# A transformer kernel on one core: head 0's first query is made before the norm's root, the modulation tiles move forward, and the first picks take other slots

## What is computed

```
mod = silu(c) @ w_ada + b_ada                      # 6 parts of 1024: shift1, scale1, gate1, shift2, scale2, gate2
h = rms_norm(x, norm1_w) * (1 + scale1) + shift1
... projections, indexed attention, short convolution -> y_mix
x = x + gate1 * (y_mix @ w_out)
h2 = rms_norm(x, norm2_w) * (1 + scale2) + shift2
# the experts, for each token and each of 8 heads:
q = h2 @ peer_wq; s = q @ subkeys                  # two halves of 128 scores
the 16 best of each half, the 16 best of their 256 sums -> 16 experts; g = softmax(of the 16 sums)
a = gelu(peer_u[expert] . h2); x += gate2 * sum(g * a * peer_v[expert])
```

## Time and profile before

| | us |
|---|---|
| three runs | 1177.68, 1178.76, 1179.75 |
| median | 1178.76 |
| the profiled execution | 1180.36 |
| its span, first to last instruction | 1178.4 |
| lies around the span | 1.96 |

### The profile page before, as it was taken

How to read it: one execution, slowest core, us unless ns; L and a number is a source line. 1 busy time by engine, 2 the same in 40 slices (tenths; PEclk the granted TensorE clock), 3 DMA queues, 4 the chain that set the end, 5 groups by cost and what they waited for, 6 DMA issues and landing times.

```text
span 1178.4 us, 18884 instructions
## 1 busy us (share of the span) xinstructions
PE 1051.1 (89%) x7587; PEld 980.2 (83%) x7587; DVE 837.5 (71%) x1801; ACT 433.0 (37%) x913; POOL 268.8 (23%) x289
## 2 busy tenths in 40 slices
PE   8999987999999987777877778878999999999997
PEld 6999986998899877777877777778899888898886
DVE  7978889667667667666776766655756868765776
ACT  3635832123212221222122122211557654476452
POOL 1000005343334333333333333434000000300000
PEclk9999999999999999998999999989999999999999
DMA  9965988999999999999999999999854655455540
GB/s 371 406 244 180 348 313 307 420 421 420 421 420 420 421 420 421 420 421 420 420 420 421 420 421 422 420 422 420 325 208 161 237 205 184 147 211 179 186 171 36
DMA packets 59480, 390.35 MB, mean 331 GB/s; under 512 B 6785, under 2 KB 7809, under 8 KB 15618
## 3 DMA queue, kind: packets, MB, share of 16 engines
q0 software_dynamic: 36864, 268.45, 55.0%
q1 hardware_dynamic: 21056, 120.10, 27.8%
q10 hardware_dynamic: 1474, 0.60, 0.2%
HBM read 388.08 MB, written 1.05 MB: 330 GB/s over the span
## 4 chain that ended last, share of the span: by engine, by line
PE 63%; DMA 24%; DVE 6%; ACT 4%; issue 1%; SPq 0%; another core or an unknown queue 0%; DVEq 0%; ACTq 0%
DMA rows<-in_peer_uv,work 23%; PE aux L1566 23%; PE pj L1609 6%; PE pj L1611 5%; PE pj L1610 5%; PE aux L1545 5%; PE pj L1286 5%; PE pj L1287 4%; PE pj L1288 4%; DVE rows L2061 2%; DMA rows<-in_w_ada 1%; PE aux L1360 1%; ACT work L1142 1%; ACT rows L1010 1%; PE aux L1425 1%
## 5 line engine op out<-in xcount | busy, mean ns | idle before, releaser
L1566 PE MATMUL aux<-work,rows 128*128 128x128 f32 x2080 | 263.4, 291 | 73.8 <-ACT work L1142 73.8
L1566 PEld LDWEIGHTS aux<-work,rows 128*128 128x128 f32 x2080 | 256.2, 206 | 81.6 <-ACT work L1142 81.4
L1566 PE MATMUL aux<-work,low_pairs 128*128 128x128 f32 x2016 | 238.2, 279 | 30.2 <-ACT work L1142 30.1
L1566 PEld LDWEIGHTS aux<-work,low_pairs 128*128 128x128 f32 x2016 | 233.0, 195 | 34.0 <-ACT work L1142 34.0
L898 POOL DMA_INDIRECT rows<-in_peer_uv,work x130 | 125.5, 965 | 301.2 <-PE aux L1566 232.1
L707 DVE TENSOR_TENSOR wlo<-wring,whi 128x1024 fp32r<-128x1024 f32 x100 | 121.0, 1235 | 77.6 <-ACT whi L701 77.1
L898 POOL DMA_INDIRECT low_pairs<-in_peer_uv,work x126 | 118.3, 939 | 158.5 <-PE aux L1566 153.4
L1286 PE MATMUL pj<-xh,whi 128*128 128x256 f32 x512 | 146.3, 286 | 0.4
L1137 ACT ACTIVATE work<-work 128x4 f32<-128x4 f32 (+2 forms) x71 | 14.7, 207 | 358.3 <-DVE work L2061 358.3
L1287 PE MATMUL pj<-xl,whi 128*128 128x256 f32 x512 | 144.8, 283 | 0.0
L1288 PE MATMUL pj<-xh,wlo 128*128 128x256 f32 x512 | 144.8, 283 | 0.0
(11 more groups left out here) (288 smaller groups left out, 1461.5 us busy)
## 6 DMA issues: line engine op xcount, KB each, us to landing
wring<-in_w SPq DMA_DIRECT2D x76, 1024.0 KB, 4.8
rows<-in_w_ada SPq DMA_DIRECT2D x40, 512.0 KB, 10.1
low_pairs<-in_w_ada SPq DMA_DIRECT2D x1, 4096.0 KB, 13.4
rows<-in_w SPq DMA_DIRECT2D x3, 1024.0 KB, 10.4
rows<-in_peer_uv,work POOLq DMA_INDIRECT x130
work<-in_late_rows SPq DMA_DIRECT2D x2, 1024.0 KB, 7.5
xT<-in_gate_rows SPq DMA_DIRECT2D x2, 1024.0 KB, 7.2
rows<-in_norm_rows SPq DMA_DIRECT2D x2, 1024.0 KB, 7.3
```

The lines of the kernel that those rows point to most:

```text
L1566: ins = mm(peer_sum[t][:, c * P:(c + 1) * P], pair(n)[:, D + c * P:D + (c + 1) * P], diag[:, n % PICKS, :], start=(n % (EXPERT_HEADS * PIC ...
```

## The change

1. `early_scores_of_head_0` is cut up. ACT makes `xT` times the gain (`times_gain`) as soon as a column of `xT` is there; PE multiplies these by head 0's query weights (`early_products`), before the root is known. DVE forms the query as product times inverted root plus the shift's part. The shift's part is made earlier: 16 products of one column (`shift_queries`), placed on PE between `sum_v` of tile 1 and `turn_y` of tile 0.
2. `second_norm` becomes one DVE multiplication of 1024 columns for each token tile, and it stands behind `route(0)`. Head 1 gets an early query too. The root for the gate's softmax is made per token (`token_sums`, `token_rms`), used in `route_pairs(0)` and `gate_exps(0)`.
3. Forty-six modulation tiles come through the ring of slots, seven more of them before the additions to `xT` begin; the last load has two tiles. The bias and gain are made before these additions.
4. The first round of picks takes slots in the order 0, 1, 6, 7, 9, 10, 11, 2, 3, 4, 8, 5 (`FIRST_ORDER`), and so do all rounds up to pick 239; picks 240 and up use n % 12 again.

```diff
-ADA_AFTER = {4: range(16, 21), 7: (21, 22), 8: (23, 24), 9: (25, ), 13: range(26, 29), 18: range(29, 34), 22: (34, ), 20: (35, ), 25: (36, 37), 27: (38, 39)}
+ADA_AFTER = {4: range(16, 21), 7: (21, 22), 8: (23, 24), 9: (25, ), 12: range(26, 31), 13: range(31, 34), 14: (34, 35), 18: range(36, 41), 22: (41, ), 20: (42, ),
+             25: (43, 44), 27: (45, )}
+RING_TILES = 46
...
+FIRST_ORDER = (0, 1, 6, 7, 9, 10, 11, 2, 3, 4, 8, 5)
+LAST_ROUND = LAST_PICK // SLOTS * SLOTS - SLOTS
+def slot(n):
+    return n % SLOTS if n >= LAST_ROUND else FIRST_ORDER[n % SLOTS]
+def pick_ahead_in_slot(n):
+    return max(m for m in range(n - 2 * SLOTS, n) if m >= 0 and slot(m) == slot(n))
...
-                    sp.wait_ge(sums, 1 + NT)
+                    sp.wait_ge(sums, 2 + NT)
...
+                    if n >= SLOTS:
+                        pool.wait_ge(pair_used, pick_ahead_in_slot(n) + 1)
+                    elif k in FIRST_QUERY_SLOTS:
+                        pool.wait_ge(queries, 2 * FIRST_QUERY_SLOTS.index(k) + 2)
+                    elif k == KEYS_SLOT:
                         pool.wait_ge(expert_scores, 2)
-                    if n == LAST_ADA_SLOT:
-                        pool.wait_ge(last_ada_used, KC)
-                    if n >= SLOTS:
-                        pool.wait_ge(pair_used, n - SLOTS + 1)
+                    elif k in (LAST_ADA_SLOT, CONDITION_SLOT):
+                        pool.wait_ge(last_ada_used, LAST_TILES)
...
+            def times_gain(t, c):
+                nc.scalar.activation(hT[:, c, halves_[t]], xT[:, c, halves_[t]], ACT.Copy, scale=gain[:, c:c + 1]).then_inc(gained, 1)
...
+            act.wait_ge(sums, 2 + NT)
+            nc.scalar.activation(token_rms[:, :], aux[:, 1, 0:1], ACT.Sqrt, bias=eps[:, 0:1], scale=1.0 / D).then_inc(std_ready, 1)
+            for c in range(KC):
+                times_gain(1, c)
+            shift(0)
             shift(1)
...
             sum_v(att1, pt_buf, v_of_head, tiles=(1, ))
+            first_query = UNITS_1.index(queries_of(0))
+            w_wait(pe, first_query)
+            pe.wait_ge(mod_ready, 2 * KC + 2)
+            pe.wait_ge(att1["y_out"], 1)
+            for s in range(2):
+                for k in range(KC):
+                    ins = mm(aux[:, 0, s:s + 1], w_slot(first_query)[:, k, s * P:(s + 1) * P], mod[:, 3 * KC + k:3 * KC + k + 1],
+                             start=(k == 0), stop=(k == KC - 1))
+            ins.then_inc(shift_queries, 1)
             turn_y(att1, ytok, tiles=(0, ))
...
-            out_sums(4, 5)
-            out_sums(6, 7)
+            out_sums(4, 5, tiles=(0, ))
+            early_products(*range(6))
+            out_sums(6, 7, tiles=(0, ))
+            early_products(6, 7)
+            out_sums(*range(4, KC), tiles=(1, ))
...
-            keep_busy(4, 1)
-            early_scores_of_head_0()
+            early_scores_of(0)
+            token_sums()
             pe.wait_ge(taken_dve, KC)
+            pe.wait_ge(h_ready, 2 * KC)
             turn_h2(0)
+            early_query_of_head_1()
+            early_scores_of(1)
             pe.wait_ge(h_ready, 3 * KC)
             score_query(0)
...
+            low_to(12)
+            ada_dots(21, 26)
             low_to(14)
...
+            for s in range(2):
+                dve.wait_ge(early_query, s + 1)
+                v.scalar_tensor_tensor(pq[:, 0, s, 0:P], rstd[:, 0:P], shift_query[:, s:s + 1], aux[:, 4 + s, 0:P], ALU.mult, ALU.add) \
+                    .then_inc(early_query_out, 1)
+            second_root(0)
...
             route(0)
+            for t in range(NT):
+                second_norm(t)
+                if t == 0:
+                    second_root(1)
             last_ada_tiles()
```

More of the change, by code:

```diff
@@ L1104, in score_out @@
                 act.wait_ge(expert_scores, h + 1)
-                first = 1 if h == 0 else 0
+                first = 1 if h < EARLY_HEADS else 0
                 nc.scalar.copy(s_all[:, h + first * EXPERT_HEADS::EXPERT_HEADS, :],
                                aux[:, h % 2, first * 2 * KEYS:].rearrange("p (n k) -> p n k", k=2 * KEYS)).then_inc(scores_out, 1)
-            shift(0)
-            for s in range(2):
-                act.wait_ge(early_query, s + 1)
-                nc.scalar.copy(pq[:, 0, s, 0:P], aux[:, 4 + s, 0:P]).then_inc(early_query_out, 1)
             act.wait_ge(early_scores, 1)
             nc.scalar.copy(s_all[:, 0, :], aux[:, 0, 0:2 * KEYS]).then_inc(early_scores_out, 1)
-            shift(1)
+            act.wait_ge(sums, 2 + NT)
[3 more added lines that the diff above has]
+            shift(0)
+            shift(1)
+            for s in range(2):
+                act.wait_ge(early_query, 2 + s + 1)
+                nc.scalar.copy(pq[:, 1, s, 0:P], aux[:, 4 + s, 0:P]).then_inc(early_query_out, 1)
+            act.wait_ge(early_scores, 2)
+            nc.scalar.copy(s_all[:, 1, :], aux[:, 1, 0:2 * KEYS]).then_inc(early_scores_out, 1)
             def gate_exps(g):
                 act.wait_ge(routed, g + 1)
-                nc.scalar.activation(gate[g % EXPERTS], top, ACT.Exp, bias=negtop, accum_out=gate_sum[g % EXPERTS]).then_inc(gate_exp, 1)
-            for h in range(AHEAD + 1):
-                score_query(h)
-                score_out(h)
-                if h:
-                    gate_exps(h - 1)
+                nc.scalar.activation(gate[g % EXPERTS], top, ACT.Exp, bias=negtop, scale=token_rms[:, 0:1] if g == 0 else 1.0,
+                                     accum_out=gate_sum[g % EXPERTS]).then_inc(gate_exp, 1)
+            score_query(0)
+            gate_exps(0)
+            score_out(0)
+            score_query(1)
+            score_out(1)
+            gate_exps(1)
+            score_query(2)
+            score_out(2)
             def x0_hi(t):
@@ L1512, in _, with out_sums @@
                 ins.then_inc(proj, 1)
-            def out_sums(*columns):
+            def out_sums(*columns, tiles=range(NT)):
                 for k in columns:
-                    for t in range(NT):
+                    for t in tiles:
                         pe.wait_ge(squares, k + 1 if k < KC - 1 else KC + t)
@@ L1525, in _, with early_products, token_sums @@
             whole(mixed_in, 2)
-            out_sums(4, 5)
-            out_sums(6, 7)
+            def early_products(*columns):
+                for k in columns:
+                    pe.wait_ge(gained, k + 1)
+                    for s in range(2):
+                        ins = mm(aux[:, 4 + s, 0:P], w_slot(first_query)[:, k, s * P:(s + 1) * P], hT[:, k, 0:P], start=(k == 0), stop=(k == KC - 1))
+                        if k == KC - 1:
+                            ins.then_inc(early_query, 1)
+            def token_sums():
+                pe.wait_ge(att1["y_out"], NT)
+                for k in range(KC):
+                    ins = mm(aux[:, 1, 0:1], sq[:, k, 0:P], ones[:, 0:1], start=(k == 0), stop=(k == KC - 1))
+                ins.then_inc(sums, 1)
+            out_sums(4, 5, tiles=(0, ))
[3 more added lines that the diff above has]
+            out_sums(*range(4, KC), tiles=(1, ))
             def turn_h2(t):
@@ L1555, in score_keys @@
                     pe.wait_ge(scores_out, h - 1)
-                for t in range(1 if h == 0 else 0, NT):
+                if h < EARLY_HEADS:
+                    pe.wait_ge(early_scores_out, h + 1)
+                for t in range(1 if h < EARLY_HEADS else 0, NT):
                     for s in range(2):
@@ L1778, in second_gain, with second_root, second_norm @@
                 chain.link(v.tensor_scalar(gain[:, :], part(4), 1.0, None, ALU.add))
-                chain.link(v.tensor_tensor(gain[:, :], gain[:, :], cols[:, N2W:N2W + KC], ALU.mult))
-            def second_norm():
-                for t in range(NT):
-                    ts = slice(t * P, (t + 1) * P)
-                    dve.wait_ge(std_ready, 2 + t)
-                    chain.link(v.reciprocal(rstd[:, ts], rstd[:, ts]))
-                    for c in range(KC):
-                        v.scalar_tensor_tensor(hT[:, c, ts], xT[:, c, ts], gain[:, c:c + 1], rstd[:, ts], ALU.mult, ALU.mult).then_inc(h_scaled, 1)
+                v.tensor_tensor(gain[:, :], gain[:, :], cols[:, N2W:N2W + KC], ALU.mult).then_inc(mod_ready, 1)
+            def second_root(t):
+                dve.wait_ge(std_ready, 2 + t)
+                chain.mark(v.reciprocal(rstd[:, t * P:(t + 1) * P], rstd[:, t * P:(t + 1) * P]))
+            def second_norm(t):
+                ts = slice(t * P, (t + 1) * P)
+                dve.wait_ge(gained, (t + 1) * KC)
+                chain.wait()
+                v.tensor_tensor(hT[:, :, ts], hT[:, :, ts], rstd[:, ts].unsqueeze(1).broadcast_to([P, KC, P]), ALU.mult).then_inc(h_scaled, 1)
             for z, x_in in zip((slice(0, HC), slice(HC, KC)), x_loaded):
@@ L1968, in _ @@
             y_low(1)
-            ada_dots(3 * KC + ADA_RING + 2, 4 * KC)
-            ada_dots(4 * KC, 4 * KC + 1)
-            late = 4 * KC
+            ada_dots(38, 40)
```

(2 more changed lines are left out.)

100 lines of the change are left out of this document (55 added, 45 removed).

## The result

The changed kernel takes 1196.73 us (median of 4 runs, 1196.48 to 1199.83) against 1178.96 us for the kernel before: ratio 1.0155, 95% interval 1.0143 to 1.0168. That is 17.8 us slower, where 10.0 were forecast and the range ended at 1194.5. Its profiled execution took 1196.72 us with a span of 1194.8, so the span grew by 16.4 us. The other 1.4 us lie in the kernel before: its profiled execution took 1180.36 us, 1.4 above its own median, that of the changed kernel its median. In what follows, "later" means: than the same instruction of the kernel before, in the two profiled executions.

The account below looks back on a forecast made before the run. Transfer and PE's loop were taken as coupled, the loop's later start setting the end: 11.7 + 1.5 + 1.0 - 5.0 + 0.8 = +10.0 us, median 1188.8 us, range 1184.3 to 1194.5.

Parts of the forecast that it names:

- The added wait: PE before `turn_y`: waits 7.2 us for the group's third load, then one-column products; everything after 11.7 us later.
- rival A: One-column products on PE keep the clock low: +3.4 us, 1192.2 us; chance 0.12.
- What bounds the kernel: Picks' transfer at 420 to 422 GB/s fills over half the span; its end moves only with its start and gaps.
- The clock within it: Within the added wait: four microseconds at half speed after PE's idle stretch cost 2.0 us more.
- The path to the first pick: From the last addition to routing and pick 0: routing starts 5.0 us earlier, without the added wait.
- The loop: Start of PE's loop over picks, beyond the added wait: 1.5 us later, plus 1.0 for a wait without named releaser.
- The backlog: Picks issued ahead of the transfer: slack of 5.0 us absorbs that much of the loop's later start.
- The last round: Slot order changes at pick 240, so late picks wait for slots: 0.8 us, between 0 and 1.1.
- The modulation tiles: Seven dots moved ahead of the additions fit DVE's idle time before 79.89 and 114.81 us: cost nothing.
- Rival B: The transfer, not the loop, sets the end: +5.9 us, 1184.7 us; chance 0.10.
- rival C: PE does not stand because the third load lands early: 1175.4 us (0.05) or no change (0.04); chance 0.09.
- D: Routing does not start earlier, PE's early products being behind the root anyway: 1193.8 us; chance 0.04.

Follow-up runs that it names:

- e1: The changed kernel with a semaphore of its own for the load of the first query's matrix: 1187.95 us, 1.0073.
- e4: The changed kernel with another order of the twelve row buffers in the last full round of picks: 1195.93 us, 1.0149.
- e2: The changed kernel with 36 extra large products on PE ahead of the wait for the load group, mis-sized at 15.8 us in all: 1201.99 us, 1.0185.
- e14: The changed kernel with two extra products filling PE's idle time at 68.3 us: 1197.42 us, 1.0145.
- e6: e1 with e4's buffer order, DVE's norm of tile 0 ahead of routing, and ACT's shift and gate exponentials moved ahead: 1182.74 us, 1.0033.
- e8: The changes of e6 and e7 together, on e1 with e4's buffer order: 1178.21 us, 0.9987.
- e13: The kernel before with two extra products filling PE's idle time at 68.3 us: 1177.60 us, 0.9985.
- e16: e13 with GpSimd's iota (distances) ahead of the last group's picks: 1178.79 us, 0.9992.
- e3: e1 with only 2 of the 16 one-column products: 1183.96 us, 1.0029.
- e7: e1 with e4's buffer order, the shift's part summed on VectorE and two PE products instead of 16: 1182.33 us, 1.0021.
- e12: e7 without the first query's own semaphore, its three loads sharing one: 1181.89 us, 1.0011.
- e15: e8 with early weights, PE's idle time at 68.3 us filled, and GpSimd's iota ahead of the last group's picks: 1173.19 us, 0.9944.

## Why the prediction was wrong

The direction, the place and the wait held. The step that failed is a term of the added wait, what the clock costs: 2.0 us were put down for it, and it cost about 5.5. That is what rival A said.

- **What bounds the kernel**: right. The transfer is at its limit from 260 us on in every trace, and the loop's start works through gaps in it.
- **The added wait, +11.7**: it was 16.8 at the last addition. The wait was there, on the third load of the group, behind `sum_v`'s release (e1 takes it away). The 5.0 us too little are best read from e4, whose 16.7 have no fall at 70 us in them. 1.3 are the load: the products begin at 141.39, not 140.1. 1.3 are the products: `turn_y` begins 6.84 behind their start, not 5.5. 2.1 are the half clock that the large products behind them still met (5.89 between the two `turn_y`, 3.76 before). The last 0.3 I had deducted for a wait that was to be covered. In the changed kernel's own profile the last addition is as late, but the parts are other: 1.6 by the fall at 70 us, 0.9 by the load, 1.3 by the products, 1.0 by the half clock behind them, and the 0.3.
- **The clock within it**: I put 2.0 us, four microseconds at half speed, taken from restarts with larger products. It was 3.3 to 3.4 on the products (6.98 us, against 3.63 at 1.00 in e2) and 2.1 behind them. Rival A, that short products leave the clock low, had 0.12 and +3.4 us, and that is what the runs showed: 1.3 and 2.1 more than forecast. The range let A in only with the other terms at their middle.
- **The rule on weight loads** (the Trainium skill, TensorE: Matmul & The Clock Gate, section LDWEIGHTS) would have made the term 9.6. The runs speak against it again: a weight load of the one-column products had a median of 333 ns at 0.50 and 192 ns at 1.00 (e2). Keeping the row was right.

```profile
L1534 PEld LDWEIGHTS aux<-mod,rows x32: 286/333/333, 142.6 to 149.2; 128*128 128x128 f32 x32
```

```profile
L1535 PEld LDWEIGHTS aux<-mod,rows x32: 190/192/192, 148.6 to 152.1; 128*128 128x128 f32 x32
```

- **The path to the first pick, 5.0 us earlier**: right. Routing starts 6.2 us behind the last result (6.5 forecast, 11.5 before), and pick 0 14.8 behind it (15.1 forecast, 19.8 before).
- **The loop, +1.5 and +1.0**: right in sum, 2.64 us (19.40 less 16.76; by the same reckoning 1.7 in e4 and 1.6 in e14). The 1.0 for an unnamed release was not there as such. What the step named only in passing, DVE's norm behind routing, was worth 4.0 to 4.6 us (e6, e8); PE stands 10.78 us before `turn_h2`:

```profile
195.00 1.94 PE L1603 MATMUL pj<-ident,hT 128*128 128x128 f32 x8 [10.78 <-ACT hT L1123]
```

- **The backlog, -5.0**: 4.4 (19.15 less 14.8), but part of it is not the change's. In 182:196 the profile of before moved 334 GB/s, those of e13 and e16 370 and 356 with picks issued at nearly the same times, and from pick 170 on their dots are 2.3 and 1.2 to 1.8 us ahead of its. The backlog as such may be nearer 3.
- **The last round, +0.8**: 1.6 to 1.9, with half of the cause missed. The late buffers were 1.4 (e4), but 0.9 of what they give back is lost at the iota, of which the prediction knew nothing.
- **The modulation tiles, 0**: five dots did run in the idle time before 79.9 us and two before 116.3. The clock's fall in this stretch is hardly theirs: PE's idle time ahead of it is 1.01 us in both kernels.

With the sizes measured, 16.8 + 2.6 - 4.4 + 1.6 is 16.6, against 16.4 of span. The 1.4 more between the medians are what the profile of before took above its median; that would fit the transfer that it missed in 182:196, but was not traced.

Rival B (transfer sets the end) is refuted for this kernel, rival C too, and D (routing not earlier) by the 5.0. What stays open: why the clock fell at 135.2 behind two short products and 0.20 us of idle (e3), but not behind 0.68 to 0.69 us of idle alone (before, e7, e12).

## What to carry to other kernels

A semaphore shared by several loads costs nothing for the reader of the last and the whole difference for a reader of the first; when a change moves such a reader forward, split the group or move the reader behind the last landing. Short products bound by their weight loads on the array's path should be summed on an engine with idle time first, since they also cost the clock of the work behind them. And before a wait is costed, look for the instruction far down the program that a queue issues "behind everything": it can become the limit as soon as the rest gets faster (2.5 us in e15).

## What the runs showed of the hardware

- Seven microseconds of one-column products, PE fully busy, did not raise the granted clock from 0.50; large products behind them did, after 3.2 us in the changed kernel, 5.6 in e4 and 5.4 in e14. Where the array came from full clock without idle, the same products ran at 1.00 (3.63 us in e2, 3.92 in e1), and in e1 the clock fell only at their end, to 0.50 in 137:140.
- The same program up to 76 us had the clock at 1.00 in some executions and at 0.50 for 3 to 7 us in others, around 16 two-column products and 1.0 us of idle. The Trainium skill, TensorE: Matmul & The Clock Gate, section What's actually happening, says that the chip looks at the array's activity in a rhythm of its own that doesn't start with the kernel. By that rule the clock falls at such a place or not by chance, and the traces agree: 7 of 13 without filling. With filling it was 0 of 5, which at 6 of 13 without a fall would come by chance about once in fifty times.
- A pick's issue on POOL took 1.88, 1.66 and 1.98 us at 191.5 to 197.7, while DVE ran norms and dots that read two inputs from SBUF, and 1.75 to 1.99 for the first four before (179.8 to 189.5), beside the same dots. Later issues took 0.94 to 1.02, also beside DVE's dots of picks, which read one of their inputs from PSUM (`pj`). The Trainium skill, GPSIMD Engine Reference, section Specifications, says that GpSimd shares its SBUF interfaces with VectorE, with contention for instructions with two SBUF inputs. The trace agrees.
